# Split weights at four different places modulo 256 bytes, instead of one

## The reference, cut to what matters

```
def swiglu_ffn(h, w_in, w_out):
    gate, up = jnp.split(h @ w_in, 2, axis=-1)
    return (jax.nn.silu(gate) * up) @ w_out
...
for layer in range(DEPTH):
    h = h + 0.5 * swiglu_ffn(rms_norm(h, ffn_norm[layer, 0]), ...)
    h = h + mixer(rms_norm(h, mix_norm[layer]))
    h = h + 0.5 * swiglu_ffn(rms_norm(h, ffn_norm[layer, 1]), ...)
```

## Time and profile before

| | |
|---|---|
| runs | 1876.79 us median of 3 |
| profiled execution | 1877.96 us, span 1876.2 us |
| mean granted TensorE clock | 0.989 of full |
| PE busy | 1808.3 us (96%), 18074 matmuls |
| PE weight loads busy | 1727.6 us (92%) |
| VectorE busy | 1281.0 us (68%) |
| ScalarE busy | 1034.0 us (55%) |
| DMA, queue q1 | 48.1% of 16 engines |

### The profile page before, as it was taken

How to read it: one execution, slowest core, us unless ns; L and a number is a source line. 1 busy time by engine, 2 the same in 40 slices (tenths; PEclk the granted TensorE clock), 3 DMA queues, 4 the chain that set the end, 5 groups by cost and what they waited for, 6 DMA issues and landing times.

```text
span 1876.2 us, 46612 instructions
## 1 busy us (share of the span) xinstructions
PE 1808.3 (96%) x18074; PEld 1727.6 (92%) x18074; DVE 1281.0 (68%) x2615; ACT 1034.0 (55%) x2048; POOL 25.2 (1%) x20
## 2 busy tenths in 40 slices
PE   7999999999999999999999999999989988799998
PEld 7899999999998999988889999999987887699998
DVE  6688687678686665586567664666567786557754
ACT  7656656656655554546456554655455744255553
POOL 0110000110000000000000000000000000000000
PEclk9999999999999999989999999999989999999999
DMA  7455566545564655533235566555552320036663
GB/s 247 141 155 192 159 193 181 151 140 167 153 196 135 180 178 180 168 102 92 69 96 164 179 179 178 161 178 179 179 182 90 114 69 4 4 114 190 183 187 123
DMA packets 75965, 278.08 MB, mean 148 GB/s; under 512 B 8496, under 2 KB 9904, under 8 KB 75312
## 3 DMA queue, kind: packets, MB, share of 16 engines
q1 hardware_dynamic: 75824, 276.05, 48.1%
HBM read 274.96 MB, written 1.05 MB: 147 GB/s over the span
## 4 chain that ended last, share of the span: by engine, by line
PE 82%; DVE 10%; ACT 4%; issue 3%; DMA 1%; SPq 0%; DVEq 0%; ACTq 0%
PE psum L414 23%; PE psum L415 22%; PE psum L416 22%; DVE weights_low L379 3%; ACT weights_high L371 2%; PE psum L2936 1%; DMA weight_ring<-weights_in 1%; PE psum L2568 1%; PE psum L1140 1%; PE psum L725 1%; PE psum L2913 1%; PE psum L746 1%; PE psum L554 1%; PE psum L2930 1%; DVE normed L1550 1%
## 5 line engine op out<-in xcount | busy, mean ns | idle before, releaser
L379 DVE TENSOR_TENSOR weights_low<-weight_ring,weights_high 128x512 fp32r<-128x512 f32 x984 | 663.7, 693 | 435.4 <-ACT weights_high L371 424.3
L371 ACT ACTIVATE weights_high<-weight_ring 128x512 fp32r<-128x512 f32 x984 | 604.0, 628 | 533.9 <-PE psum L416 531.6
L414 PE MATMUL psum<-ffn_normed_high,weights_high 128*128 128x272 f32 x1056 | 303.9, 288 | 3.4 <-DVE weights_low L379 2.1
L416 PE MATMUL psum<-ffn_normed_high,weights_low 128*128 128x272 f32 x1056 | 302.6, 287 | 0.0
L415 PE MATMUL psum<-ffn_normed_low,weights_high 128*128 128x272 f32 x1056 | 302.6, 287 | 0.0
L414 PE MATMUL psum<-first_normed_high,weights_high 128*128 128x256 f32 x1024 | 295.8, 289 | 3.5 <-DVE weights_low L379 2.9
L415 PE MATMUL psum<-first_normed_low,weights_high 128*128 128x256 f32 x1024 | 284.8, 278 | 0.0
L416 PE MATMUL psum<-first_normed_high,weights_low 128*128 128x256 f32 x1024 | 284.8, 278 | 0.0
L414 PEld LDWEIGHTS psum<-first_normed_high,weights_high 128*128 128x128 f32 x1024 | 193.0, 188 | 14.6 <-DVE weights_low L379 7.1
L414 PEld LDWEIGHTS psum<-ffn_normed_high,weights_high 128*128 128x128 f32 x1056 | 198.9, 188 | 5.9 <-issue 5.7
L415 PEld LDWEIGHTS psum<-ffn_normed_low,weights_high 128*128 128x128 f32 x1056 | 198.9, 188 | 0.1
(11 more groups left out here) (483 smaller groups left out, 3776.2 us busy)
## 6 DMA issues: line engine op xcount, KB each, us to landing
weight_ring<-weights_in SPq DMA_DIRECT2D x507, 512.0 KB, 3.6
arena<-first_in SPq DMA_DIRECT2D x1, 2176.0 KB, 10.8
consts<-const_in SPq DMA_DIRECT2D x1, 1895.0 KB, 7.6
arena<-vec_in SPq DMA_DIRECT2D x1, 1536.0 KB, 10.5
arena<-vec_in SPq DMA_DIRECT2D x1, 1152.0 KB, 5.9
residual<-x_in SPq DMA_DIRECT2D x2, 544.0 KB, 4.9
out<-normed SPq DMA_DIRECT2D x4, 256.0 KB, 2.4
weight_ring<-weights_in SPq DMA_DIRECT2D x2, 256.0 KB, 5.1
```

The costliest lines, as they stand in the source:

```text
L371: nc.scalar.activation(WH[:, n % SPLIT, half], W[:, n % RING, half], ACT.Copy).then_inc(weights_high, 1)
L379: nc.vector.tensor_tensor(WL[:, n % SPLIT, half], W[:, n % RING, half], WH[:, n % SPLIT, half].bitcast(F32), ALU.subtract).then_inc(weight ...
L414: nc.tensor.matmul(psum, WH[:, s, cols], high, start=start, stop=False)
L416: return nc.tensor.matmul(psum, WL[:, s, cols], high, start=False, stop=stop)
```

## The change

Each place of `WH` and `WL` gets a row of 1040 elements (4160 bytes) instead of 1024, and the last 16 elements are cut away by a slice. Nothing else is edited; no instruction is added, removed or moved.

```
-        WH, WL = sb("weights_high", [P, SPLIT, D], F32R), sb("weights_low", [P, SPLIT, D], F32R)
+        WH, WL = (sb("weights_high", [P, SPLIT, D + 16], F32R)[:, :, 0:D], sb("weights_low", [P, SPLIT, D + 16], F32R)[:, :, 0:D])
```

## The result

The changed kernel takes 1890.99 us, the median of 3 runs (1890.16 to 1891.75), against 1876.79 us: a ratio of 1.0079, 95% interval 1.0061 to 1.0097. It is slower by 14.2 us. Its profiled execution has a span of 1888.4 us, 12.2 us more than that of before.

A forecast was written before the change was run, and what follows sets the result against it. PE's matmul pitch was taken to bound the kernel, the split being paced by PE. 10.5 us (272 columns) plus 11 us (256 columns), others 0, made +21.5 us on 1876.8: 1898 us, range 1869 to 1913.

The forecast's parts named there:

- The mechanism: In PE's matmuls, row streaming and the next weight load collide at some distances modulo 256 bytes, costing 7 to 13 ns each.
- 272 columns, rows alike: 4752 matmuls of ffn_normed and ffn_inner whose rows don't step: +2.2 ns each, 10.5 us, with ends of 4.8 and 13.3.
- 256 columns, rows alike: 4224 matmuls of first_normed, first_raw and branches, whose rows don't step: 11 us more, the middle of 7.2 and 14.4.
- Stepping rows: last_*, mixer, mixed and rwkv_* meet all four distances before and after, only reordered: 0, within 3.3 us either way.
- The splits: L371 and L379, which read and write the moved places, keep 628 and 693 ns: 0, or 3.2 us either way without cover.
- Nothing takes the loss up again: Across the kernel, PE hardly waits, so the whole +21.5 us was expected to show in the time.
- all distances behave as stepping rows do: Upper end for the 256-column matmuls with rows alike: 3 to 5 ns more each, 14.4 us.
- the even blocks keep what they have: Lower end for 256-column matmuls with rows alike: two of three even-block loads keep distance 64, leaving half, 7.2 us.
- no change: Rival for the whole kernel: the moving row's own place causes the extra, so the time stays 1877 us; chance 0.14.
- Faster: Rival: alternating WH and WL loads, 128 bytes apart, hold pe_tile's reads in a good position, 1859 us; chance 0.18.
- the second term: The forecast sum's 11 us for the 256-column matmuls whose rows don't step.
- the first term: The forecast sum's 10.5 us for the 272-column matmuls whose rows don't step.

The follow-up runs named there:

- e1: Kernel before with all four places of the split weights 192 bytes behind the unstepped rows, modulo 256, instead of 64; 1899.93 us, ratio 1.0115.
- e2: Kernel before with all four places of the split weights 128 bytes behind the unstepped rows instead of 64; 1903.61 us, ratio 1.0130.
- e3: Kernel before with all four places of the split weights at the same place modulo 256 as the unstepped rows (distance 0); 1899.26 us, ratio 1.0112.
- e5: Kernel before with all four places of the split weights 96 bytes behind the unstepped rows instead of 64; 1889.06 us, ratio 1.0058.
- e6: Kernel before with all four places of the split weights 32 bytes behind the unstepped rows instead of 64; 1900.53 us, ratio 1.0111.
- e12: Kernel before with all four places of the split weights 80 bytes behind the unstepped rows instead of 64; 1901.99 us, ratio 1.0131.
- e4: Kernel before with weights and everything behind them moved together by 128 bytes, so distances stay; 1876.38 us, ratio 0.9997.
- e7: Kernel before with both places of the low weights at distance 192 bytes, the high ones kept at 64; 1880.15 us, ratio 1.0014.
- e8: Kernel before with the rows of the last feed-forward block at 1280 bytes instead of 1088, so they don't step; 1872.48 us, ratio 0.9972.

## Why the prediction was right, point by point

- **The mechanism** holds as far as it was tested. A matmul's pitch depends on where its row and the weights stand to each other modulo 256 bytes: all other constant distances tried are slower in the whole (e1 to e3, e5, e6, e12), and moving both leaves the time (e4). That two reads get in one another's way, and that at half clock they go at like speed and so stay apart, is a reading of this that no run looks into; and at 256 columns the distance does not fix the pitch alone.
- **272 columns, rows alike**: forecast +2.2 ns; measured 125.7 - 123.3 = 2.4 ns in the long stretch, 2.2 and 2.0 ns as the means of `ffn_normed` and `ffn_inner`, and 10.0 us of PE's busy time in the three blocks against a forecast of 10.5. Right, though the table of lengths in the earlier trace rows from which one end came does not hold (e1).
- **256 columns, rows alike**: forecast 11 us, measured 7.1 us of PE's busy time in the first stack. This is the term that was mis-sized. I took the middle between "all distances behave as stepping rows do" and "the even blocks keep what they have". The second is what happened: even blocks stay at 276 ns, and e7, in which all blocks are laid out as the even ones, has `branches` at 113.3 ns and `first_normed` at a mean of 114.1; that end was 7.2 us.
- **Stepping rows**: forecast 0 within 3.3 us; the last block took 0.8 us more, and the mean pitch of `mixer` fell from 126.1 to 125.4 ns. Right.
- **The splits**: forecast no price; 694 and 628 ns. Right.
- **"Nothing takes the loss up again"**: this was wrong by a little. PE's idle time in the first stack and the three blocks shrank by 2.3 us, among it its waits for L379 (12.2 to 9.8 us): a slower PE finds the next split ready more often. The 3.5 us that the mixer and the recurrence lost in the profile are another thing, the clock of that execution.
- **The rivals**: "no change" and the Trainium skill's rule behind it ("SBUF — State Buffer", section "Who interferes with whom") are refuted by e1 to e4: the address of weights against rows alone takes PE from 123.3 to 126.7 ns and the kernel from 1877 to 1904 us, where the rule leaves no room for a difference. Which part of the chip makes the one wait is not seen. "Faster" rested on a good position at 192 bytes that doesn't exist. The Trainium skill's start-to-start ("TensorE: Matmul & The Clock Gate", section "Wait — 56ns, not 53.3ns?"), 109.2 and 115.8 ns, was not reached by full stretches of `pe_tile` here in any run; the best were 113.3 and 123.3.

The whole came to 14.2 us instead of 21.5, inside the range and on the forecast side. Of the 7.3 us that are missing the second term is 3.9, the first 0.5, and the idle time that was taken up 2.3; the rest is within what single executions differ by. That the sum came so near is in part luck: the first term was a choice between an end taken from lengths, which e1 shows to be no measure, and the pitch of `mixer`.

## What to carry to other kernels

Where TensorE reloads weights for every matmul, the pitch of equal matmuls is worth comparing between tensors: a few nanoseconds times many thousands of matmuls are visible, and they can hang on the distance of the two operands modulo 256 bytes. Measure a distance by holding it constant in a whole run, not by reading it off rows that change it. Take a mean over many stretches, for a single one can run in another of two pitches. A row length that is a multiple of 256 bytes lets one good distance serve all rows (here 118.3 to 113.4 ns in `last_normed`, 0.28% of the kernel); then try the distances. Spreading buffers over different places gave about the average of good and bad ones.

## What the runs showed of the hardware that was not expected

- Over seven constant distances the pitch has no smooth course. At 272 columns (one stretch of `ffn_normed`) for 0, 32, 64, 80, 96, 128, 192 bytes: 125.4, 126.6, 123.3, 126.6, 123.3, 126.6, 126.7 ns; at 256 columns (`branches` of the second layer): 120.0, 118.2, 113.3, 118.6, 118.6, 120.0, 117.9 ns.
- At one distance and with the same addresses, matmuls of 256 columns run at 113.3 or at 117.8 ns and keep that for a whole block or longer, up to some 430 matmuls (e8's `last_inner`; also the earlier trace rows). The two occur at distances of 64 and of 192 bytes, in other shares.
- At half clock the effect is absent: 226.7 ns for 272 columns, exactly the streaming.
